# Layer norm statistics moved to ScalarE and PSUM, final norm in pieces: a two-layer streaming encoder step on one core

## What is computed

```python
y = depthwise_conv(v) + b_dw
y = silu(layernorm(y, g_ln, b_ln))     # mean and variance over the 1024 channels
out = (y * silu(z)) @ w_out            # 1024 x 1024, "output projection" of layer 0
h = h + rmsnorm(out, g_post[0])
...
out = (o * silu(z)) @ w_b_out          # 1024 x 1024, last product of layer 1
h = h + rmsnorm(out, g_post[1])        # "final norm", h is y_out
```

## Time and profile before

| | |
|---|---|
| median of 3 runs | 617.22 us (616.61 to 619.89) |
| profiled execution | its own time 619.28 us, span from first to last instruction 617.5 us |
| busy share of the span | PE 88%, DVE 71%, ACT 50%, POOL 49% |
| mean granted TensorE clock | 0.969 of full |

### The profile page before, as it was taken

The page is one execution under the profiler, slowest core; times in us unless marked ns, Lnnn a source line. Parts: engine busy times, 40 slices in busy tenths (PEclk is TensorE's granted clock), DMA queues, the critical chain, the costliest instruction groups (busy, mean ns, idle before and its releaser), DMA issues.

```text
span 617.5 us, 10866 instructions
## 1 busy us (share of the span) xinstructions
PE 544.1 (88%) x4056; PEld 494.8 (80%) x4056; DVE 438.5 (71%) x848; ACT 306.0 (50%) x734; POOL 299.6 (49%) x275
## 2 busy tenths in 40 slices
PE   1899999988993899989999997899999998779981
PEld 0899999988772799879999996767877786479980
DVE  4886999999998848788387024766867867750066
ACT  6744456466466954644444334454455356354230
POOL 4748888889994931666729512011111112215033
PEclk9999999999998999999999998999999999969995
DMA  7423313331204400440313331200110121101012
GB/s 244 123 84 89 87 58 105 84 89 42 86 20 119 137 29 2 118 137 1 102 53 103 110 94 25 75 29 2 45 62 1 54 86 52 51 1 53 2 54 91
DMA packets 31397, 43.17 MB, mean 70 GB/s; under 512 B 5840, under 2 KB 21744, under 8 KB 31344
## 3 DMA queue, kind: packets, MB, share of 16 engines
q1 hardware_dynamic: 31344, 42.47, 23.2%
HBM read 37.25 MB, written 3.10 MB: 65 GB/s over the span
## 4 chain that ended last, share of the span: by engine, by line
PE 50%; DVE 32%; ACT 5%; issue 4%; SPq 3%; POOL 3%; DMA 2%; DVEq 0%; ACTq 0%
PE ps L429 13%; DVE ps L973 13%; PE ps L431 12%; PE ps L430 12%; PE ps L1675 3%; PE ps L1716 2%; DVE probs L1226 2%; PE ps L1696 2%; ACT probs L816 2%; SPq L492 2%; POOL rtop_lo L420 1%; DVE rowmax L1199 1%; DVE ps L900 1%; DVE zs L1278 1%; DVE xT L1281 1%
## 5 line engine op out<-in xcount | busy, mean ns | idle before, releaser
L420 POOL TENSOR_TENSOR rlow_lo<-stage,rlow_hi 128x384 fp32r<-128x384 f32 (+2 forms) x88 | 98.2, 1128 | 213.3 <-ACT rlow_hi L414 213.3
L429 PE MATMUL ps<-act_hi,rlow_hi 128*128 128x272 f32 (+1 forms) x368 | 110.4, 300 | 19.9 <-issue 8.8
L973 DVE SCALAR_TENSOR_TENSOR ps<-v,vecs,ps 128x574 f32<-128x574 f32 x162 | 118.4, 811 | 0.0
L429 PE MATMUL ps<-act_hi,rtop_hi 128*128 128x272 f32 x384 | 112.0, 292 | 3.6 <-DVE v L944 2.2
L431 PE MATMUL ps<-act_hi,rtop_lo 128*128 128x272 f32 x384 | 111.1, 289 | 0.0
L430 PE MATMUL ps<-act_lo,rtop_hi 128*128 128x272 f32 x384 | 110.5, 288 | 0.0
L431 PE MATMUL ps<-act_hi,rlow_lo 128*128 128x272 f32 (+1 forms) x368 | 107.1, 291 | 0.0
L430 PE MATMUL ps<-act_lo,rlow_hi 128*128 128x272 f32 (+1 forms) x368 | 106.9, 291 | 0.0
L429 PEld LDWEIGHTS ps<-act_hi,rlow_hi 128*128 128x128 f32 (+1 forms) x368 | 69.6, 189 | 23.9 <-issue 11.1
L429 PEld LDWEIGHTS ps<-act_hi,rtop_hi 128*128 128x128 f32 x384 | 72.2, 188 | 4.8 <-DVE v L944 2.7
L420 POOL TENSOR_TENSOR rtop_lo<-stage,rtop_hi 128x384 fp32r<-128x384 f32 (+1 forms) x56 | 64.4, 1168 | 23.7 <-ACT rtop_hi L414 23.7
(11 more groups left out here) (186 smaller groups left out, 1252.8 us busy)
## 6 DMA issues: line engine op xcount, KB each, us to landing
stage<-w_in SPq DMA_DIRECT2D x64, 192.0 KB, 2.6
stage<-w_bi SPq DMA_DIRECT2D x24, 256.0 KB, 2.7
stage<-w_ao SPq DMA_DIRECT2D x16, 256.0 KB, 2.9
stage<-w_bo SPq DMA_DIRECT2D x16, 256.0 KB, 2.8
stage<-w_qb SPq DMA_DIRECT2D x16, 192.0 KB, 2.6
xT<-x_t SPq DMA_DIRECT2D x4, 544.0 KB, 5.7
y_out<-xT SPq DMA_DIRECT2D x16, 136.0 KB, 1.8
stage<-w_kb SPq DMA_DIRECT2D x8, 256.0 KB, 2.7
```

The costliest lines, as they stand in the source:

```text
L420: nc.gpsimd.tensor_tensor(l, stage[:, u % STAGES, 0:unit_cols(u)], h.bitcast(F32), ALU.subtract).then_inc(lo_done, 1)
L429: nc.tensor.matmul(out, wh, xh, start=start, stop=False)
L973: ins = nc.vector.scalar_tensor_tensor(out=dst, in0=src, scalar=tap, in1=dst, op0=ALU.mult, op1=ALU.add)
```

## The change

Layer norm: mean squared is made by ACT from the mean's PSUM bank, variance and clamp stay in the PSUM bank of the squares, the copy of the mean is gone; PE finishes half 0's squares before it begins half 1. ACT makes the high parts of U_AO+5 to U_AO+7 before it squares tile 7. Three of the units U_AO+8 to U_AO+15 (`AO_EARLY`) are split before the tile loop, on ACT behind the load of the Silu table, on POOL ahead of the first rest; the other five follow n + 1 = 2, 4, 6, 8 and 9.

Final norm: half 1's sums are made in pieces inside products 13, 14 and 15, and one piece behind product 15; the last fold is gone. Products 12 to 15 (half 1, tiles 4 to 7) stay in PSUM and are scaled there with the gain. DVE writes the scaled tiles to PSUM; the tiles are split anew between DVE and POOL, and the stores follow the new order.

```diff
-POOL_FINAL = 5
-AO_AFTER = (1, 2, 3, 4, 5, 6, 7, 8)
+FINAL_DVE, FINAL_POOL = ((0, 1, 2, 3), (4, 5, 6, 7, 3)), ((4, 5, 6, 7), (0, 1, 2))
+Y_ORDER = ((0, 4, 1, 5, 2, 3, 6, 7), (4, 0, 5, 6, 1, 7, 3, 2))
+F_EVACS = 12
+FSTAT_SLOTS = {13: (0, 1, 4), 14: (5,), 15: (2,)}
+AO_EARLY = 3
+AO_AFTER = (2, 4, 6, 8, 9)
...
             for j in range(KD - 1):
                 gate_silu(j)
-                if j < STAGES:
-                    hi(act, U_AO + j)
+                hi(act, U_AO + j)
             load_table(ACT.Sqrt)
+            hi(act, U_AO + KD - 1)
...
+            def mean_square(b):
+                act.wait_ge(ymean_done, b + 1)
+                nc.scalar.activation(rstd_b[:, blk(b)], ps[:, YMEAN[b], 0:HB], ACT.Square, scale=1.0 / D).then_inc(msq_done, 1)
+            mean_square(0)
             evac_z(KD - 1)
-            for u in range(U_AO + STAGES, U_AO + KD):
-                hi(act, u)
+            mean_square(1)
...
-                sqrt_of(N_LN + b, b)
+                act.wait_ge(var_done, N_LN + b + 1)
+                nc.scalar.activation(var_b[:, blk(b)], ps[:, YSQ[b], 0:HB], ACT.Sqrt).then_inc(sqrt_done, 1)
             load_table(ACT.Silu)
+            for i in range(AO_EARLY):
+                hi(act, U_AO + KD + i)
...
-                nc.scalar.activation(zs[:, m, blk(b)], ps[:, n % 4, 0:HB], ACT.Copy,
-                                     scale=vecs[:, V_POST1 + m:V_POST1 + m + 1]).then_inc(f_evac, 1)
+                if n < F_EVACS:
+                    nc.scalar.activation(zs[:, m, blk(b)], ps[:, n % 4, 0:HB], ACT.Copy,
+                                         scale=vecs[:, V_POST1 + m:V_POST1 + m + 1]).then_inc(f_evac, 1)
...
             def moments(b):
-                n = link(nc.vector.tensor_scalar(mean_b[:, s], ps[:, YMEAN[b], 0:HB], 1.0 / D, None, ALU.mult))
-                n = link(nc.vector.tensor_tensor(rstd_b[:, s], mean_b[:, s], mean_b[:, s], ALU.mult))
...
-                nc.vector.tensor_scalar(var_b[:, s], var_b[:, s], 0.0, EPS, ALU.max, ALU.add).then_inc(var_done, 1)
+                sums = ps[:, YSQ[b], 0:HB]
+                dve.wait_ge(msq_done, b + 1)
+                dve.wait_ge(ystat_done, b + 1)
+                n = link(nc.vector.scalar_tensor_tensor(out=sums, in0=sums, scalar=1.0 / D, in1=rstd_b[:, blk(b)],
+                                                        op0=ALU.mult, op1=ALU.subtract))
+                dve.wait_ge(dve_self, n)
+                nc.vector.tensor_scalar(sums, sums, 0.0, EPS, ALU.max, ALU.add).then_inc(var_done, 1)
...
+                    if b and m >= 4:
+                        dve.wait_ge(fsq_done, 2 * KD)
+                        out = ps[:, m - 4, 0:HB]
+                        return out, link(nc.vector.scalar_tensor_tensor(
+                            out=out, in0=out, scalar=vecs[:, V_POST1 + m:V_POST1 + m + 1], in1=rstd,
+                            op0=ALU.mult, op1=ALU.mult))
+                    out = ps[:, 6 + i % 2, 0:HB]
...
+                    return out, link(nc.vector.tensor_tensor(out, zs[:, m, blk(b)], rstd, ALU.mult))
...
+                    nc.vector.tensor_tensor(xT[:, m, blk(b)], part_of, xT[:, m, blk(b)], ALU.add).then_inc(y_done, 1)
-                if b == 0:
-                    fold(fsq[:, 1, 0:2, :], fsq[:, 1, 4:6, :], fsq_done, 14, fsum_done, 2)
...
+            for i in range(AO_EARLY):
+                lo(pool, U_AO + KD + i)
             for n in range(2 * KD):
                 rest(y[:, k, blk(b)], act_hi[:, k, blk(b)], act_lo[:, k, blk(b)], n + 1, yz_lo, yz_hi)
...
             for b in range(NB):
+                if b:
+                    ysum(mean, ysums[:, 0, blk(b)], True)
+                ysum(mean, y[:, KD - 1, blk(b)], False).then_inc(ymean_done, 1)
+                ysum(squares, ysums[:, 1, blk(b)], True)
                 pe.wait_ge(ysq_done, KD + b)
+                ysum(squares, sq[:, 2 + b, :], False).then_inc(ystat_done, 1)
...
+            def fstat1(slots, last=False):
...
+                    ins = nc.tensor.matmul(ps[:, 5, 0:HB], ones[:], fsq[:, 1, i, :], start=i == 0, stop=last)
...
+                    if n in FSTAT_SLOTS and k == KD // 2:
+                        fstat1(FSTAT_SLOTS[n])
...
-            fstat(1)
+            fstat1((3,), True).then_inc(fstat_done, 1)
```

More of the change, by code:

```diff
@@ L141, with final_count @@
 FTASKS = [(m, b) for c in range(2) for b in range(2) for m in range(4 * c, 4 * c + 4)]
+def final_count(tiles, b, m):
+    return len(tiles[0]) * b + tiles[b].index(m) + 1
 def evacs(eng, n):
@@ L674, in _ @@
                 if n in AO_AFTER:
-                    hi(act, U_AO + KD + AO_AFTER.index(n))
+                    hi(act, U_AO + KD + AO_EARLY + AO_AFTER.index(n))
                 if n >= 12:
@@ L1272, in _, with scale @@
                 inverse(N_F + b, rstd_b, b)
-                dve.wait_ge(f_evac, (12, 16)[b])
-                for m in range(POOL_FINAL + 1):
-                    if m < POOL_FINAL:
-                        at = link(nc.vector.tensor_tensor(zs[:, m, blk(b)], zs[:, m, blk(b)], rstd_b[:, blk(b)], ALU.mult))
-                    if m:
-                        dve.wait_ge(dve_self, before)
-                        nc.vector.tensor_tensor(xT[:, m - 1, blk(b)], xT[:, m - 1, blk(b)], zs[:, m - 1, blk(b)],
-                                                ALU.add).then_inc(y_done, 1)
-                    before = at
-                if b == 0:
-                    fold(fsq[:, 1, 0:2, :], fsq[:, 1, 4:6, :], fsq_done, 14, fsum_done, 2)
+                dve.wait_ge(f_evac, F_EVACS)
+                tiles = FINAL_DVE[b]
+                def scale(i, b=b, tiles=tiles):
+                    m = tiles[i]
+                    rstd = rstd_b[:, blk(b)]
+                    if b and m >= 4:
[5 more added lines that the diff above has]
+                    out = ps[:, 6 + i % 2, 0:HB]
+                    if i >= 2 and not b:
+                        dve.wait_ge(y_done, i - 1)
+                    return out, link(nc.vector.tensor_tensor(out, zs[:, m, blk(b)], rstd, ALU.mult))
+                following = scale(0)
+                for i, m in enumerate(tiles):
+                    part_of, at = following
+                    if i + 1 < len(tiles):
+                        following = scale(i + 1)
+                    dve.wait_ge(dve_self, at)
+                    nc.vector.tensor_tensor(xT[:, m, blk(b)], part_of, xT[:, m, blk(b)], ALU.add).then_inc(y_done, 1)
         @block.gpsimd
@@ L1381, in _ @@
                 if n + 1 in AO_AFTER:
-                    lo(pool, U_AO + KD + AO_AFTER.index(n + 1))
+                    lo(pool, U_AO + KD + AO_EARLY + AO_AFTER.index(n + 1))
             def xn_rest(n):
@@ L1512, in _, with ysum @@
                     last.then_inc(mt_done, 1)
-            def ysum(bank, src, first):
-                return nc.tensor.matmul(ps[:, bank, 0:HB], ones[:], src, start=first, stop=not first)
+            def ysum(out, src, first):
+                return nc.tensor.matmul(out, ones[:], src, start=first, stop=not first)
             pe.wait_ge(fold_done, folds(KD - 2))
-            ysum(YMEAN[0], ysums[:, 0, blk(0)], True)
+            ysum(ps[:, YMEAN[0], 0:HB], ysums[:, 0, blk(0)], True)
             pe.wait_ge(y_ready, KD)
-            ysum(YMEAN[0], y[:, KD - 1, blk(0)], False).then_inc(ymean_done, 1)
-            ysum(YMEAN[1], ysums[:, 0, blk(1)], True)
-            ysum(YMEAN[1], y[:, KD - 1, blk(1)], False).then_inc(ymean_done, 1)
             for b in range(NB):
-                ysum(YSQ[b], ysums[:, 1, blk(b)], True)
+                mean, squares = ps[:, YMEAN[b], 0:HB], ps[:, YSQ[b], 0:HB]
+                if b:
+                    ysum(mean, ysums[:, 0, blk(b)], True)
+                ysum(mean, y[:, KD - 1, blk(b)], False).then_inc(ymean_done, 1)
+                ysum(squares, ysums[:, 1, blk(b)], True)
                 pe.wait_ge(ysq_done, KD + b)
-                ysum(YSQ[b], sq[:, 2 + b, :], False).then_inc(ystat_done, 1)
+                ysum(squares, sq[:, 2 + b, :], False).then_inc(ystat_done, 1)
             def product(bank, units, m, b, kts, stats=None, fresh=None):
@@ L1776, in _ @@
                 if n == 12:
[L1777 to L1778 removed]
+                    fstat0()
+            fstat1((3,), True).then_inc(fstat_done, 1)
 def kernel(x_prompt, x_sample, state_conv, cache_kv_latent, cache_k_rope,
```

52 lines of the change are left out of this document (25 added, 27 removed).

## The result

The changed kernel takes **611.98 us** (median of four runs, 611.17 to 613.31) against 618.17 for the kernel before in the same comparison: ratio 0.9896, 95% interval 0.9871 to 0.9921. It is faster by some 6 us where 8.75 were forecast; 611.98 lies inside the range and 3.5 us above the forecast. By its time alone it is nearer to what rivals 1 and 2 were to give (611.2 and 612.9), so only the pieces of the profile can decide. The profiled execution took 613.31 us, with a span of 611.6.

What follows compares the result with a forecast made beforehand. POOL's weight splits ahead of the output projection and the uncovered end were taken to bound the kernel. Layer norm 4.35 plus end 4.4 gave 8.75 us, median 617.22 to 608.5 us; range 606.5 to 613.0.

Steps and rivals of the forecast that it cites:

- Rival 1: Final norm: DVE and POOL hold each other up also with PSUM operands; end gains 1.7, 611.2 us; chance 0.09.
- rival 2: Layer norm: first rest waits for ACT's copies or late POOL splits, using up the 4.35; 612.9 us; chance 0.10.
- What bounds the kernel: POOL's weight splits between rests delay PE before the output projection; at the program's end nothing hides anything.
- Layer norm, head: Up to the first rest: reciprocal 1.3 us earlier, but three early splits put the rest at 199.95 against 199.64.
- Layer norm, pace: Through the eighth rest: fewer splits, PE nearly the bound, product 3 at 211.15 instead of 215.50, 4.35 us gained.
- bound of 3.3 us: Lower bound of the layer norm's gain, if PE's clock comes back 2 us later.
- POOL bound of the forecast: Upper bound of the layer norm's gain, 4.8 us, if POOL alone paces; product 3 at 210.7.
- Rival 3: PE's clock stays at 1.2 GHz after the pause until about 228 us; slower, 621 us; chance 0.03.
- no later than before in effect: Layer norm head: half 0's second statistic sum on PE done at about 190.8, claimed to cost nothing.
- Final norm, sums: Half 1's sums: five of six go into products 13 to 15, 2.35 us of PE; reciprocal 1.85 us earlier.
- at no cost: Final norm, half 0's new split: DVE 5.7 us, POOL 7.8 us, both covered until half 1's reciprocal at 605.6.
- Final norm, tail: After half 1's reciprocal: PSUM operands avoid the DVE-POOL hold-up; last store 610.9 against 615.27, 4.4 us including 1.85 from sums.

Runs made afterwards that it cites:

- the second execution: The changed kernel once more, no edit: 612.79 us, ratio 0.9926 to the kernel before.
- filler products: Changed kernel with 14 products of ones, result unused, put into PE's pause ahead of the first rest: 611.67 us, ratio 0.9877.
- the tail in SBUF: Changed kernel with DVE's scaled tiles of the final norm written to SBUF instead of PSUM: 612.76 us, ratio 0.9917.
- the block: Changed kernel with half 1's final sums as before, a fold and four products behind product 15: 609.78 us, ratio 0.9869.
- the copies in ACT's waits: Changed kernel with the three early high parts of U_AO+8 to U_AO+10 moved to where ACT waits anyway: 611.44 us, ratio 0.9896.

## Why the prediction was right and wrong

**What bounds the kernel** was read rightly: POOL's splits between the rests, and the bare end. Taking the splits out let PE run 10.00 of 10 us, and what was saved at the 8th output product was still saved at the 16th.

**Layer norm, head: right.** The first rest was to come 0.31 us later, and came 0.32 later (2.01 in the second execution, where the clock fell among the sums). The two parts stand too: 1.23 to 1.26 us from the statistics (forecast 1.3), 1.55 for the three splits ahead of it. ACT's copies waited for no load, so rival 2 fell as to its cause.

**Layer norm, pace: this is the step that failed.** It charged 13 passes at the lower clock, 1.3 us, taken from the stretch of the kernel before. There the clock had come back at 203.31 us, 2.8 us after PE's restart. In the changed kernel it came back 4.8 us after it. 21 passes ran at that level, at a price of 4.87 - 2.6 = 2.2 us: 0.9 more than charged, which is the miss of 4.35 - 3.39 = 0.96 within the reading. This is the case for which the prediction gave its bound of 3.3 us, a clock that comes back 2 us later, and the bound held this profile. In all four profiles with this layer norm and without filler products the low level lasted 4.4 to 5.0 us beyond the restart (three of them with the fall among the sums), so the length read from the kernel before didn't carry over. The bound did not hold the second execution, with 1.63: there the fall among the sums, which no bound had, took another 1.69 at the first rest. That the step hung on the clock is shown by the filler products: with them alone the gain was 4.24. It would then have been expected to go above 4.35, as no pass is slow; but rests now come in pairs, and PE has 18 passes left after the first of the last pair, not nine, so it ends some 0.5 us later than the POOL bound of the forecast. Rival 3, the slower clock, was thus right in its kind and not in its size: 0.9 to 2.6 us, not 12. What the prediction set against it, that PE now works more densely, did not bring the clock back sooner: PE was busy 3.00 of 3.00 us from 203 to 206, at 0.50.

Why the clock falls among the sums in some executions is not settled. It did so in four of seven profiles in which PE pauses 0.78 us for the squares (the second execution, the tail in SBUF, the block, the copies in ACT's waits) and in none of seven where it pauses less or not at all. The pause came from the change itself: ACT's copies ahead of the squares hold up half 0's last sum, and half 1's sums now wait behind it, which the prediction let pass as "no later than before in effect". That the pause is the cause fits all of this; no run changed the pause alone.

**Final norm, sums: right in size, wrong in its account.** Forecast 1.85, measured 1.79; the inserted products took 2.32 us of PE (forecast 2.35), the last square to the reciprocal 2.15 (forecast 2.10). But the prediction booked half 0's scales and adds "at no cost" and without a gain, at 5.7 us of DVE for four tiles; they took 595.80 - 591.86 = 3.94. With the scales in PSUM, half 0 ends 3.0 us sooner behind its reciprocal than with the same split in SBUF (5.82 for 8.82; the split by itself brings 0.15). This removes the wait for the fold, and with it the reason for the pieces: with the block the sums end 1.65 us sooner than with the pieces, in three profiles (41.00 to 41.05 for 42.68 to 42.74). What the pieces hid was gone, and what was left was their price.

**Final norm, tail: right.** 2.40 for 2.55, with POOL last, as forecast. The adds took 0.427 us and the scales from PSUM 0.500, with POOL busy beside them. Rival 1 is refuted, and writing to SBUF, with the same split, brings the hold-up back. One reading was wrong, without weight in the sum: the 0.496 us of a scaling is not the price of its PSUM output, for the scales from PSUM with the gain took 0.491 into SBUF and 0.500 into PSUM. The Trainium skill (GPSIMD Engine Reference, section 8, Key points) says that GpSimd contends with VectorE instructions that have two SBUF inputs. The traces agree. In POOL's timeline of the changed kernel its scale beside DVE's work on PSUM took 0.76 us, its next add, beside tile 3's scale, 0.96:

```profile
606.27 0.76 POOL L1474 TENSOR_TENSOR zs<-zs,rstd_b 128x272 f32<-128x272 f32 x1
606.99 0.96 POOL L1479 TENSOR_TENSOR xT<-xT,zs 128x272 f32<-128x272 f32 x1
```

The price is seen on both engines. Tile 3's scale, with two SBUF inputs, ends at 606.77 + 0.57 = 607.34, 0.31 us behind POOL's scale (606.27 + 0.76 = 607.03). It lost some 0.14 us because it began late in POOL's scale. One scale of half 0, which began 0.3 us into POOL's, took 1.02. So the four others' 0.45 to 0.57 come from the moment at which they began and not from their output in PSUM: in the run with the tail in SBUF two adds took 0.58 with their output in SBUF.

**The sum.** The end's terms gave 4.3 us for 4.4. The layer norm gave 1.6 or 3.4 for 4.35. With 3.0 us of the first block of sums in the profile of before perhaps 1.0 too long, the end is worth 3.3 to 4.3 on the run of executions. That makes 4.9 to 7.7, and the two comparisons of the changed kernel, 0.9896 and 0.9926, are 6.4 and 4.6 us, the second 0.3 below. That the time came into the range was helped by the range's reach: its upper end was set by the rivals and not by the bounds of the forecast, which gave 607.4 to 610.2.

## What to carry to other kernels

When a change makes an engine the bound, look at what its slow stretch cost while it was waiting anyway: that cost moves onto the path. If it rests on the clock, the length seen in the kernel before need not hold in the changed one: it must be given a range, or be removed (here by products nobody reads, in the pause). Cost a cover together with what it covers: pieces that hide a wait are a loss as soon as another part of the same change takes the wait away. And put early copies where the engine waits anyway: there the same three cost the first rest nothing that could be seen, where behind the table load they had cost 1.55 us.

## What the runs showed of the hardware

- After PE's pause ahead of the first rest (6.6 to 10.4 us without work) the lower clock level lasted another 2.8 to 5.0 us beyond the restart in the nine profiles without filler products: 2.8 and 3.1 in the two with the layer norm of before, 4.4 to 5.0 in the four with the changed one. The Trainium skill (TensorE: Matmul & The Clock Gate, Part 1) says that the number of slow products after a kernel's start varies from run to run. No run here bears on a kernel's start. After this pause in the middle of a kernel the two executions of the changed kernel differ by 0.16 us, and most of the spread of 2.2 us lies between programs.
- In the four of these profiles in which PE restarted 3.8 to 4.0 us behind the fall of the clock, the low level lasted 6.8 us in all; in the five in which it restarted 5.3 to 7.0 us behind it, 10.2 us. No run varied this alone.
- Products of ones that nobody reads kept the granted clock at 1.00 through this pause, in all five profiles that had them.
- A DVE scale or add of the final norm with two SBUF inputs that begins while POOL is at work ends 0.29 to 0.31 us behind POOL's instruction, so it takes from 0.55 us (begun late in it) to 1.02 us (begun early); without POOL beside it 0.43. Whether it writes to SBUF or PSUM made no difference. With one input in PSUM it was not held up: 0.42 to 0.43 us for an add.
